# Moving the low halves and the split weights 128 bytes up in SBUF

## The reference

```
first block:  even layer  h = rmsnorm(x); proj = h @ w_in (1024 x 6144); conv + two gated linear
                          recurrences + gated short conv; x + rmsnorm(y @ w_out)
              odd layer   gated linear attention, 4 heads, both directions, chunks of 64
second block: layer 0     h + 0.5*swiglu; stick-breaking attention, 16 heads; h + 0.5*swiglu;
                          then shared keys and values (compressed, selected, window)
              layer 1     h + 0.5*swiglu; attention over three branches; h + 0.5*swiglu
swiglu(x) = (silu(a) * b) @ w_out,  a, b = split(x @ w_in),  2816 hidden features
```

## Time and profile before

| | |
|---|---|
| median of 3 runs | 2854.99 us (2854.55 to 2858.11) |
| the profiled execution | 2856.48 us, span 2854.6 us |
| TensorE busy, its weight loads | 2753.4 us, 2191.4 us |
| GpSimd, VectorE, ScalarE busy | 1636.4, 1371.0, 698.3 us |
| mean granted clock of TensorE | 0.981 of full |

### The profile page before, as it was taken

The page is one execution under the profiler, slowest core; times in us unless marked ns, Lnnn a source line. Parts: engine busy times, 40 slices in busy tenths (PEclk is TensorE's granted clock), DMA queues, the critical chain, the costliest instruction groups (busy, mean ns, idle before and its releaser), DMA issues. The chain is left out here.

```text
span 2854.6 us, 35943 instructions
## 1 busy us (share of the span) xinstructions
PE 2753.4 (96%) x13128; PEld 2191.4 (77%) x13128; DVE 1371.0 (48%) x1588; ACT 698.3 (24%) x1190; POOL 1636.4 (57%) x952
## 2 busy tenths in 40 slices
PE   7999989988899999988999999999999999999999
PEld 5777777756688888856888888788888766788887
DVE  8878823462641453046642346643246466543141
ACT  4433422232310111066210011311012266311010
POOL 4666755503566665610666665666566588666565
PEclk9999999988999999999999999999999899999999
DMA  4222222201232232300333232423232100133232
GB/s 174 97 89 95 89 81 89 74 1 54 79 107 88 92 103 89 96 30 1 96 96 109 85 105 83 133 96 111 81 103 89 52 2 1 59 94 117 78 99 85
DMA packets 62026, 235.63 MB, mean 83 GB/s; under 512 B 6880, under 2 KB 7008, under 8 KB 61792
## 3 DMA queue, kind: packets, MB, share of 16 engines
q1 hardware_dynamic: 61920, 234.21, 25.6%
HBM read 232.08 MB, written 2.10 MB: 82 GB/s over the span
## 5 line engine op out<-in xcount | busy, mean ns | idle before, releaser
L305 POOL CAST w_hi<-ring 128x1024 fp32r<-128x1024 f32 (+2 forms) x396 | 451.8, 1141 | 1088.5 <-PE ps L325 788.6
L307 POOL TENSOR_TENSOR w_lo<-ring,w_hi 128x1024 fp32r<-128x1024 f32 (+2 forms) x396 | 1021.1, 2578 | 57.9 <-issue 2.4
L323 PE MATMUL ps<-hi,w_hi 128*128 128x512 f32 x2128 | 836.0, 393 | 7.5 <-DVE lo L1451 3.9
L325 PE MATMUL ps<-hi,w_lo 128*128 128x512 f32 x2128 | 830.2, 390 | 0.0
L324 PE MATMUL ps<-lo,w_hi 128*128 128x512 f32 x2128 | 829.8, 390 | 0.0
L323 PEld LDWEIGHTS ps<-hi,w_hi 128*128 128x128 f32 x2128 | 400.7, 188 | 97.9 <-DVE lo L1451 5.5
L324 PEld LDWEIGHTS ps<-lo,w_hi 128*128 128x128 f32 x2128 | 400.7, 188 | 84.6 <-issue 2.4
L325 PEld LDWEIGHTS ps<-hi,w_lo 128*128 128x128 f32 x2128 | 400.5, 188 | 83.9
L323 PE MATMUL ps<-hid_hi,w_hi 128*128 128x512 f32 x704 | 274.4, 390 | 0.0
L325 PE MATMUL ps<-hid_hi,w_lo 128*128 128x512 f32 x704 | 273.9, 389 | 0.0
L324 PE MATMUL ps<-hid_lo,w_hi 128*128 128x512 f32 x704 | 273.9, 389 | 0.0
(11 more groups left out here) (303 smaller groups left out, 3273.6 us busy)
## 6 DMA issues: line engine op xcount, KB each, us to landing
ring<-in_ffn_in SPq DMA_DIRECT2D x176, 512.0 KB, 3.5
ring<-in_even_in SPq DMA_DIRECT2D x48, 512.0 KB, 4.4
ring<-in_ffn_out SPq DMA_DIRECT2D x32, 768.0 KB, 4.2
ring<-in_ffn_out SPq DMA_DIRECT2D x32, 640.0 KB, 3.8
ring<-in_even_out SPq DMA_DIRECT2D x16, 512.0 KB, 3.5
ring<-in_odd_v SPq DMA_DIRECT2D x8, 512.0 KB, 3.5
ring<-in_odd_r SPq DMA_DIRECT2D x8, 512.0 KB, 3.5
ring<-in_odd_qk SPq DMA_DIRECT2D x8, 512.0 KB, 3.5
```

The costliest lines, as they stand in the source:

```text
L305: nc.gpsimd.tensor_copy(w_hi[:, j % 2, 0:cols], ring[:, j, 0:cols])
L307: nc.gpsimd.tensor_tensor(w_lo[:, j % 2, 0:cols], ring[:, j, 0:cols], w_hi[:, j % 2, 0:cols].bitcast(F32), ALU.subtract).then_inc(sem["w_r ...
L323: nc.tensor.matmul(bank, w_hi[:, j % 2, w], x_hi[:, k, :], start=(start and k == 0), stop=False)
L325: mm = nc.tensor.matmul(bank, w_lo[:, j % 2, w], x_hi[:, k, :], start=False, stop=(stop and k == kt - 1))
```

## The change

FREE grows from 19840 to 19872 floats. All that stands behind the first FREE floats of the arena moves 128 bytes up: `lo`, `w_hi`, `w_lo`, `w_raw`, `w_tails`, `kstn`, the states, `pr`. Nothing else moves, and no instruction is added or taken away. `lo` and the weights are then at 96 modulo 256 in the count above, `hi` and the tiles in the arena still at 224.

```diff
@@ -120,7 +120,7 @@
         def tiled(name, n, cols, start, dt=F32):
             return at(name, n * cols, start, dt)[:, :].rearrange("p (k t) -> p k t", t=cols)
 
-        FREE = 19840
+        FREE = 19872
         ARENA = FREE + DT * T + 4 * SLOT
         for name, cols in (("consts", (N_CONSTS + 7) // 8 * 8), ("small", 16), ("masks", 2 * P), ("res", DT * T),
                            ("hi", DT * T), ("ring", RING * SLOT), ("root", T), ("rinv", T), ("acc", T), ("arena", ARENA)):
```

## The result

The changed kernel takes 2891.73 us (median of 4, 2887.68 to 2896.17), the kernel before beside it 2856.05 us (2854.55 to 2858.11). The ratio is 1.0124, with a 95% interval of 1.0112 to 1.0137: 35.7 us slower. I had forecast 2855 and a range from 2805 to 2869.

What follows compares the result with a forecast made beforehand. TensorE's wide float32r matmuls were taken to bound the kernel, 10,080 x 226.7 ns, 80% of the span. All terms were 0: 2854.6 + 0 = 2854.6, forecast as 2855 us, range 2805 to 2869.

Steps and rivals of the forecast that it cites:

- What bounds the kernel: Whole kernel: TensorE is busy 96% of the span; 10,080 wide float32r matmuls take 80%, a nanosecond on each 10.1 us.
- Wide matmuls: Term for float32r matmuls of 512 columns: 7600 change distance to 128 bytes, at 0 ns each.
- The bound for a loss: Worst case for the 7600 matmuls, from line 828's 256- and 384-column matmuls: up to 3.8 ns each, 29 us.
- the lonely matmul: Matmul at 369.9 us with no weight load following: 388 ns against 389, so 9 of 10 ns were the moving stream's.
- D: Rival, slower: distance 0 is the good phase; up to 3.8 ns x 7600 = +29 us, 2884; chance 0.19.
- B: Rival, faster: today's small overlap with the weight load vanishes at 128 bytes; -8 to -15 us, 2843; chance 0.14.
- C: Rival, faster: the whole 10.2 ns surplus is a bank conflict and goes; up to -78 us, 2777; chance 0.17.
- The pairing: In product, each matmul pairs with the load beside it: lines 323 and 325 get distance 128, line 324 stays at 0.
- GpSimd, VectorE, attention, DMA at 0: Terms for GpSimd's splits, VectorE's lo, attention and gated part's plain float32 streams, and DMA targets: 0 us each.

Runs made afterwards that it cites:

- micro: Separate small program, not the kernel: only float32r matmuls, 48 per distance of weights from moving operand; 226.7 ns pitch at distance 0, 233.3 at 128.
- micro2: Separate small program again, with fewer weight columns, more distances, and pairs whose second matmul has no load beside it; those second matmuls took 387 to 398 ns.
- lo_only: Against the kernel before: lo 128 bytes up and the weights 256 up, so only lo moves modulo 256; 2886.08 us, ratio 1.0103.

## Why the prediction was wrong

- *What bounds the kernel.* Right. TensorE's stream of wide float32r matmuls set the time, a nanosecond on each is some 10 us, and there was no second lever: waits and other engines moved nothing.
- *The failed step: "Wide matmuls. ... Value taken: 0 ns each."* Measured 34.0 us over all wide lines, 4.5 ns for each of the 7600 matmuls, or 35.7/7600 = 4.7 from the medians. The bound for a loss, 3.8 ns, was too low as well. It came from narrow matmuls that by the listing stand at distance 0 too, so it could not tell what another distance costs; and its excess of 3.8 came from sharing the surplus out by columns, where micro shows it to be 13.3 ns per matmul at 256, 384 and 512 columns. Width even changes the sign: at 256 columns distance 128 is the faster one, 118.7 against 120.0 ns.
- *What led to it.* "If the load cost 10 ns, the lonely matmul would be 10 ns shorter. It is 1 ns shorter". That compares two matmuls at distance 0, where the stream runs in its best pattern. At best it could tell what a load at distance 0 adds; it says nothing of another distance. And it was one sample, with one check: micro2 has lone matmuls from 387 to 398 ns at any distance. "So 9 of the 10 ns belong to the stream of the moving operand itself" is shown by no run.
- *Rivals.* D was right in its sign and its place: distance 0 is the good phase, and its mark, 391 ns or more, came on lines 323 and 325. Its argument against, that GpSimd, VectorE and DMA leave TensorE at 389 ns, did not bear on it: they are other readers, and the stream alone shows the effect. Its price of 29 us was 7 short. B and C fell: at 128 nothing is won, and no distance tried wins at 512 columns. The argument I used against B, that the two reads advance at different speeds so that the start does not stay what it was, would have denied any effect. The start distance does decide.
- *The pairing.* Line 324 as untouched and 323 as hit came true in the mean (225.9 and 232.5), but not as a rule. Line 325, counted as hit, pays 1.4 ns; line 341 and, with lo, 585 and 586, whose moving operand had moved along with what is loaded beside it, were counted as untouched and pay some 5. In lo_only two lines at distance 0 pay as well. A matmul's pitch hangs on its neighbours too. Leaving out the steps of 753 to 755, some 5,700 matmuls pay 5 to 8 ns, where I had 7600 at up to 3.8: count and price of D erred in opposite directions, and that its 29 us came so near is in part luck.
- *GpSimd, VectorE, attention, DMA at 0.* Right. No wait grew by 1 us in the rows shown, the cast on GpSimd still waits 648.8 us for line 325 (636.5 before), and plain float32 has 429.1 and 429.2 ns at the two distances.
- The Trainium skill's pages "SBUF — State Buffer" (section "SBUF: two separate sides") and "TensorE: Matmul & The Clock Gate" (section "What happens when you issue a matmul") would have both operands read independently. The micro run differs for float32r, with 226.7 against 233.4 ns and nothing else at work, and the measurement decides; for bf16 and plain float32 no run here differs.

**Shown:** the start distances of weights and moving operand modulo 256, in their order, set the pitch of wide float32r streams, up to the choice among a few patterns; no other engine and no DMA is needed for it; only the relative distance counts. **Open:** which reads meet inside the chip, if it is that; how much of the 13.3 ns at distance 0 is the load's; why 240 and 252 are as good as 0 while 248, 4 and 8 are not; and what picks the pattern when a stretch begins.

## What to carry to other kernels

Keep moving operand and stationary weights (128 columns) of float32r matmuls of 384 or 512 columns a multiple of 256 bytes apart, in every pair of a step; after any change of a tile's size or an arena's, count the distances again, for here 128 bytes cost 1.2% and 64 bytes 2.1%. A trace in which every pair has one setting says nothing of the others, however tight its durations: then a program of a few dozen matmuls by itself is worth more than any inference. And a lone instruction is a poor stand-in for a steady stream, whose cost is a pattern of many.

## What the runs showed of the hardware that I had not expected

- Float32r, 512 columns, 128 columns of weights, full clock: 226.7 ns at the distances 0, 240, 252, 256 and 512; 229 to 234 at the others tried. Bf16: 215.8 at four distances. Plain float32: 429.1 and 429.2 at two.
- At distance 0 the pitch is 120.0, 173.3 and 226.7 ns for 256, 384 and 512 columns: 13.3 ns above the columns at 2.4 GHz each time. So that surplus is per matmul and not per column, as I had shared it out. At 128 and 192 columns the pitch is 111.7 ns at either distance, so it isn't the moving columns that set it; that the load does is likely and not shown.
- The disturbed pitch is not one value. In lo_only 228.9, 231.1 and 233.3 ns stand in long stretches of the same code, 6.7 ns apart per step of three, and the two stretches shown keep theirs to the end.
